# A fused two-block kernel: how the first four feed-forward units follow the second norm

## The reference, cut to what matters

```
x = x + gt_a * rmsnorm_2(mix @ w_out[l], g_post_attn[l])

h = rmsnorm_2(x, g_pre_ffn[l]) * (1.0 + sc_f) + sh_f
f = (jax.nn.silu(h @ w_gate[l]) * (h @ w_up[l])) @ w_down[l]
x = x + gt_f * rmsnorm_2(f, g_post_ffn[l])
```

## Time and the profile before

| | us |
|---|---|
| median of 3 runs (lowest, highest) | 3028.91 (3028.78, 3029.4) |
| profiled execution, own time | 3028.81 |
| its span | 3027.1 |
| TensorE busy in it | 3009.3 (99%) |
| VectorE busy | 2268.5 (75%) |
| ScalarE busy | 1244.6 (41%) |
| GpSimd busy | 361.5 (12%) |

### The profile page before, as it was taken

The page is one execution under the profiler, slowest core; times in us unless marked ns, Lnnn a source line. Parts: engine busy times, 40 slices in busy tenths (PEclk is TensorE's granted clock), DMA queues, the critical chain, the costliest instruction groups (busy, mean ns, idle before and its releaser), DMA issues.

```text
span 3027.1 us, 41400 instructions
## 1 busy us (share of the span) xinstructions
PE 3009.3 (99%) x15360; PEld 2532.1 (84%) x15360; DVE 2268.5 (75%) x2840; ACT 1244.6 (41%) x1596; POOL 361.5 (12%) x523
## 2 busy tenths in 40 slices
PE   9999999999999999999999999999999999999998
PEld 7888887888888888888888788888888888888887
DVE  7666656868887666788765798888888888888875
ACT  5332343213234333444442454444444444344433
POOL 0211100111110011010000200000000000011123
PEclk9999999999999999999999999999999999999999
DMA  5444453876764444444332366666666666578874
GB/s 193 151 127 133 136 196 135 322 261 232 263 250 169 162 166 167 146 154 154 138 140 97 119 180 171 179 178 176 180 173 170 173 168 179 186 228 229 229 228 158
DMA packets 121373, 544.43 MB, mean 180 GB/s; under 512 B 22496, under 2 KB 22768, under 8 KB 81584
## 3 DMA queue, kind: packets, MB, share of 16 engines
q1 hardware_dynamic: 64432, 321.15, 30.1%
q0 software_dynamic: 53088, 194.85, 23.3%
q10 hardware_dynamic: 3744, 26.98, 2.3%
HBM read 433.86 MB, written 37.49 MB: 156 GB/s over the span
## 4 chain that ended last, share of the span: by engine, by line
PE 98%; DVE 2%; DMA 0%; ACT 0%; issue 0%; DVEq 0%; SPq 0%; ACTq 0%
PE PS L2007 18%; PE PS L1553 15%; PE PS L1554 15%; PE PS L1555 15%; PE PS L2010 9%; PE PS L2077 3%; PE PS L2076 3%; PE PS L2074 3%; PE PS L2042 1%; PE PS L2044 1%; PE PS L2043 1%; PE PS L1876 1%; PE PS L1612 1%; PE PS L1614 1%; PE PS L1613 1%; PE PS L1864 1%
## 5 line engine op out<-in xcount | busy, mean ns | idle before, releaser
L1553 PE MATMUL PS<-XHL,WH 128*128 128x512 f32 x1952 | 765.0, 392 | 0.3 <-DVE BB L2581 0.3
L1555 PE MATMUL PS<-XHL,WL 128*128 128x512 f32 x1952 | 759.9, 389 | 0.0
L1554 PE MATMUL PS<-XHL,WH 128*128 128x512 f32 x1952 | 759.6, 389 | 0.0
L986 ACT ACTIVATE WH<-RAW 128x2048 fp32r<-128x2048 f32 x137 | 262.1, 1913 | 463.4 <-PE PS L1555 461.9
L1553 PEld LDWEIGHTS PS<-XHL,WH 128*128 128x128 f32 x1952 | 366.5, 188 | 80.7 <-issue 4.0
L1555 PEld LDWEIGHTS PS<-XHL,WL 128*128 128x128 f32 x1952 | 366.4, 188 | 76.5
L1554 PEld LDWEIGHTS PS<-XHL,WH 128*128 128x128 f32 x1952 | 366.6, 188 | 74.8 <-issue 0.2
L2093 DVE TENSOR_TENSOR WL<-RAW,WH 128x2048 fp32r<-128x2048 f32 x136 | 310.9, 2286 | 66.9 <-ACT WH L986 66.7
L1341 ACT ACTIVATE QH<-RAW 128x1024 fp32r<-128x1024 f32 x210 | 222.2, 1059 | 251.7 <-PE PS L2010 242.6
L2007 PE MATMUL PS<-XHL,QH 128*128 128x512 f32 x1008 | 316.6, 395 | 0.0
L2954 DVE TENSOR_TENSOR QL<-RAW,QH 128x1024 fp32r<-128x1024 f32 x210 | 256.6, 1222 | 58.6 <-ACT QH L1341 58.4
(11 more groups left out here) (446 smaller groups left out, 5277.2 us busy)
## 6 DMA issues: line engine op xcount, KB each, us to landing
RAW<-w_units_dram SPq DMA_DIRECT2D x228, 1024.0 KB, 4.9
ADA<-w_ada_dram POOLq DMA_DIRECT2D x112, 512.0 KB, 5.5
ADAQ<-w_ada_dram POOLq DMA_DIRECT2D x80, 512.0 KB, 5.6
A<-w_units_dram SPq DMA_DIRECT2D x32, 1024.0 KB, 7.8
SUM<-RAW POOLq DMA_DIRECT2D x42, 512.0 KB, 4.7
RAW<-SUM POOLq DMA_DIRECT2D x42, 512.0 KB, 4.5
FRAW<-f_dram SPq DMA_DIRECT2D x4, 2048.0 KB, 13.0
A<-A POOLq DMA_DIRECT2D x8, 1024.0 KB, 7.5
```

What stands on the lines that cost most here:

```text
L986: act.activation(WH[:, slot, :], RAW[:, slot, :], ACT.Copy).then_inc(hi_ready, 1)
L1553: pe.matmul(PS[:, bank, :], wh, rh[:, x, :], start=k == 0, stop=False)
L1554: pe.matmul(PS[:, bank, :], wh, rl[:, x, :], start=False, stop=False)
L1555: ins = pe.matmul(PS[:, bank, :], wl, rh[:, x, :], start=False, stop=k == n - 1)
```

## The change

Units 0, 1 and 2 run in step: tile k of unit 0, tile k - 1 of unit 1 and tile k - 1 of unit 2. Unit 2's weights move to slot 1 of `WH`/`WL` and are prepared during the norm; unit 3's move to `PAIRH`/`PAIRL` and are prepared in halves, and its output goes to bank 5. The tiles pass through three PSUM banks where there were four, so a norm step from tile 3 on also waits for ScalarE's copy of the tile three before it (`x_copied`). The `scaled_by_row` steps stand later: after the low step, and at other tiles (`SCALED_AT`). GpSimd makes the first combination of `RES`, in eight pieces of 128x256 behind its additions 8 to 15; VectorE makes the others in a new order. The saves of `BB` to DRAM go from ScalarE's queue to SP's, the table load for silu goes ahead of the tiles, one sum of the norm is folded on VectorE so that TensorE has four small matmuls fewer, and the second block of dummy matmuls has six instructions where it had four. SP loads the two weights of the second fast pair behind unit 3 instead of unit 1, the second of them behind GpSimd's first accumulating DMA.

```diff
@@ constants
+SCALED_AT = {1: (5, 7), 3: (7, 9), 6: (9, 11), 8: (11, 13), 10: (13, 16)}
-    XBANK = (2, 3, 4, 6)
+    XBANK = (3, 4, 6)
+    UPBANK = (1, 5)
@@ SP
+            x3_save(0, 4)
             for k in range(2):
+                if k == 1:
+                    for t0, t1 in ((4, 8), (8, 12), (12, 14), (14, 16)):
+                        x3_save(t0, t1)
                 sp.wait_ge(lo_ready, U_FFN + 3 + k)
                 sp.dma_start(RAWS[0][:, k, :], w_units[U_FFN + 2 * PLAIN + k]).then_inc(pair_loaded[0], 16)
-            sp.wait_ge(out_done, O_FFN + 2)
+            sp.wait_ge(out_done, O_FFN + 4)
             for k in (1, 0):
+                if k == 0:
+                    sp.wait_ge(later_sums, 16)
                 sp.dma_start(RAWS[1][:, k, :], w_units[U_FFN + 2 * PLAIN + 2 + k]).then_inc(pair_loaded[1], 16)
@@ GpSimd
                 gp.tensor_tensor(BB[:, t, :], BB[:, t, :], RES[:, t, :], ALU.add).then_inc(x3_ready, 1)
+                if t >= FULL_K:
+                    k = t - FULL_K
+                    gp.wait_ge(x_copied, k + 1)
+                    ins = gp.tensor_tensor(RES[:, k, LO], RES[:, k, LO], RES[:, k, HI], ALU.subtract)
+            ins.then_inc(t_sum, 1)
@@ ScalarE
+            act.activation(WH[:, 1, :], RAW[:, 0, :], ACT.Copy).then_inc(hi_ready, 1)
 ...
+            act.activation(SPARE, ONES[:, 0:1], ACT.Silu)
             for t in range(DT):
                 act.wait_ge(x_freed, DT + t + 1)
-                act.activation(XH[:, t, :], PS[:, XBANK[t % 4], :], ACT.Identity,
+                act.activation(XH[:, t, :], PS[:, XBANK[t % 3], :], ACT.Identity,
                                bias=MOD[:, 3 * DT + t:3 * DT + t + 1]).then_inc(xh_ready, 1)
                 if t >= 1:
-                    x_copied(t - 1)
-                if t % 4 == 3:
-                    act.wait_ge(x3_ready, t + 1)
-                    act.dma_start(x3_d[:, t - 3:t + 1, :], BB[:, t - 3:t + 1, :]).then_inc(saved, 16)
-            x_copied(DT - 1)
-            third_hi(act, U_FFN + 2, 2, 0)
-            act.activation(SPARE, ONES[:, 0:1], ACT.Silu)
+                    x_copy(t - 1)
+            fourth_hi(0)
+            x_copy(DT - 1)
@@ TensorE
-            token_sums(SIG[:, 1, :], 0, G2[:, DT - 1:DT], False, True, bank=4)
-            clocked(4, 0, O_OUT2 + DT - 1)
+            clocked(6, 0, O_OUT2 + DT - 1)
-            pair(U_FFN, O_FFN, X_FFN, True)
-            third(U_FFN + 2, O_FFN + 2, 3, 2, X_FFN)
-            unit(U_FFN + 3, 1, O_FFN + 3, [FULL], 3, 4, X_FFN)
+            for k in range(TILES + LAG):
+                if k < TILES:
+                    paired(0, k, U_FFN, X_FFN, own=True)
+                if k >= LAG:
+                    ins = paired(1, k - LAG, U_FFN, X_FFN, own=True)
+                    if k - LAG == TILES // 2 - 1:
+                        ins.then_inc(half_used, 1)
+                    if k == LAG:
+                        pe.wait_ge(half_lo, 7)
+                    if k - LAG == TILES // 2:
+                        pe.wait_ge(lo_ready, U_FFN + 3)
+                    ins = product(WH[:, 1, :], WL[:, 1, :], 2, k - LAG)
+            ins.then_inc(out_done, 1)
+            pe.wait_ge(half_lo, 8)
+            for k in range(TILES):
+                if k == TILES // 2:
+                    pe.wait_ge(lo_ready, U_FFN + 4)
+                ins = product(PAIRH, PAIRL, UPBANK[1], k)
+            ins.then_inc(out_done, 1)
@@ VectorE
-            scaled_by_row(5, 7)
+            home_lo(WH[:, 1, :], WL[:, 1, :], RAW[:, 0, :], 0, None)
             v.wait_ge(row_ready, 4)
             for t in range(DT + 1):
                 if t < DT:
                     v.wait_ge(x3_ready, t + 1)
+                    if t >= 3:
+                        v.wait_ge(x_copied, t - 2)
 ...
-                if t in (1, 3, 5):
-                    scaled_by_row(t + 6, t + 8)
-                if t == 7:
-                    scaled_by_row(13, 16)
                 if t >= 1:
 ...
+                if t in SCALED_AT:
+                    scaled_by_row(*SCALED_AT[t])
+                if t == 4:
+                    home_lo(WH[:, 1, :], WL[:, 1, :], RAW[:, 0, :], 1, U_FFN + 3)
+            home_lo(PAIRH, PAIRL, RAW[:, 1, :], 0, 6)
```

More of the change, by code:

```diff
@@ L411, in build @@
         saved, misc_loaded = sem("saved"), sem("misc_loaded")
+        x_copied, x3_saved = sem("x_copied"), sem("x3_saved")
         rope_ready, vt_ready, vtr_done, vs_ready, qk_done = (
@@ L421, in build @@
         x2_loaded = [sem(f"x2_loaded{c}") for c in range(4)]
[L422 to L425, removed]
+        last_square, prod_ready, u_ready = (sem(n) for n in ("last_square", "prod_ready", "u_ready"))
+        turn_ready, turn_saved, gate_moved, gained, root_ready, corner_scaled, corner_added = (
+            sem(n) for n in ("turn_ready", "turn_saved", "gate_moved", "gained",
                              "root_ready", "corner_scaled", "corner_added"))
@@ L1464, in _ @@
             ins.then_inc(t_hi, 1)
+            fourth_hi(1)
+            plain_silu(0)
             plain_silu(1)
@@ L1970, in _ @@
             token_sums(SIG[:, 1, :], 0, ONES[:, 0:1], False, True).then_inc(ms_ready, 1)
-            token_sums(ACCC, 0, ONES[:, 0:1], True, False, bank=4)
+            token_sums(ACCB, 4, ONES[:, 0:1], True, False, bank=4)
             token_rows(3, 0, 7)
-            token_sums(ACCB, 4, ONES[:, 0:1], False, False, bank=4)
-            token_sums(SIG[:, 1, :], 0, G2[:, DT - 1:DT], False, True, bank=4)
             pe.wait_ge(prod_ready, 1)
+            token_sums(ACCC, 0, ONES[:, 0:1], False, True, bank=4)
+            pe.wait_ge(prod_ready, 2)
             token_sums(PROD, 4, ONES[:, 0:1], False, True, bank=4).then_inc(ms_ready, 1)
@@ L2013, in fast_pair, with product @@
                     ins.then_inc(q_done, 1)
-            pair(U_FFN, O_FFN, X_FFN, True)
-            third(U_FFN + 2, O_FFN + 2, 3, 2, X_FFN)
-            unit(U_FFN + 3, 1, O_FFN + 3, [FULL], 3, 4, X_FFN)
+            def product(wh, wl, bank, x):
+                wh, wl = wh[:, x * P:(x + 1) * P], wl[:, x * P:(x + 1) * P]
+                pe.matmul(PS[:, bank, :], wh, XH[:, x, :], start=x == 0, stop=False, skip_group_check=True)
+                pe.matmul(PS[:, bank, :], wh, XL[:, x, :], start=False, stop=False, skip_group_check=True)
+                return pe.matmul(PS[:, bank, :], wl, XH[:, x, :], start=False, stop=x == TILES - 1,
+                                 skip_group_check=True)
+            for u in range(2):
+                pe.wait_ge(out_read, READ0 + O_FFN + u - 1)
+            for k in range(TILES + LAG):
[17 more added lines that the diff above has]
+            ins.then_inc(out_done, 1)
             with pe.Fori(0, LOOPED // 4) as i:
@@ L2890, in _ @@
                     modulation(V_GPF, 4 * DT)
+                    v.tensor_tensor(DS, MOD[:, 3 * DT:3 * DT + FULL_K], MOD[:, 3 * DT + FULL_K:4 * DT], ALU.subtract)
+            v.drain()
+            v.wait_ge(last_square, 1)
+            v.scalar_tensor_tensor(out=ACCC[:, :], in0=SIG[:, 1, :], scalar=G2[:, DT - 1:DT], in1=ACCC[:, :],
+                                   op0=ALU.mult, op1=ALU.add).then_inc(prod_ready, 1)
             v.wait_ge(out_read, READ0 + O_FFN)
@@ L2918, in _ @@
             tt(m, m, AE, ALU.add)
-            ts(e, m, EPS, None, ALU.max).then_inc(mean_ready, 1)
+            ts(e, m, EPS, None, ALU.max).then_inc(prod_ready, 1)
             scaled_by_row(4, 5)
@@ L2922, in _, with home_lo @@
             v.reciprocal(e, e).then_inc(scale_ready, 1)
-            scaled_by_row(5, 7)
+            def home_lo(hi, lo, raw, h, count):
+                part = slice(h * D // 2, (h + 1) * D // 2)
+                v.wait_ge(hi_ready if h or count is None else half_hi, U_FFN + 3 if count is None else count)
+                v.tensor_tensor(lo[:, part], raw[:, part], f32(hi[:, part]), ALU.subtract)\
+                 .then_inc(lo_ready if h else half_lo, 1)
+            home_lo(WH[:, 1, :], WL[:, 1, :], RAW[:, 0, :], 0, None)
             v.wait_ge(row_ready, 4)
@@ L3107, in _, with third_t @@
             ins.then_inc(t_lo, 1)
+            def third_t(tiles):
+                for t in tiles:
+                    m = 3 * DT + FULL_K + t
+                    ins = v.scalar_tensor_tensor(out=TC[:, t, hi], in0=RES[:, FULL_K + t, hi], scalar=MOD[:, m:m + 1],
+                                                 in1=f32(TC[:, t, lo]), op0=ALU.add, op1=ALU.subtract)
+                return ins
+            lo_part(0, 0, 0, 0)
             sum_3(0, 32)
-            lo_part(0, 0, 0, 0)
+            sum_1(0)
             lo_part(0, 0, 1, 1)
-            sum_1(0)
+            lo_part(0, 0, 2, 2)
+            plain_hidden(0)
             plain_hidden(1)
             v.drain().then_inc(copied, 1)
-            lo_part(0, 0, 2, 2)
             lo_part(0, 0, 3, 3)
             v.wait_ge(t_hi, 3)
-            for t in range(FULL_K):
-                m = 3 * DT + FULL_K + t
```

(4 more changed lines are left out.)

57 lines of the change are left out of this document (30 added, 27 removed).

## The result

| | before | after |
|---|---|---|
| median, us (lowest to highest, 20 runs each) | 3029.02 (3028.58 to 3029.63) | 3032.93 (3031.37 to 3034.82) |
| ratio after / before, 95% interval | | 1.0013 (1.0007 to 1.0019) |
| span of the profiled execution | 3027.1 | 3031.3 |

A forecast was written before the change was run, and what follows sets the result against it. The prediction took TensorE as the bound, busy 3009.3 of 3027.1 us. From the profiled 3028.81 it subtracted 3.6 for the earlier first fast pair and took all else at 0: 3025.2, range 3024.0 to 3028.0.

The forecast's parts named there:

- The first fast pair earlier by 3.6: With three units in step, the first fast pair starts at 1760.8 us instead of 1764.39.
- The wait between tile 0 and tile 1: TensorE's waits on the low step shrink from 4.7 to about 1.5 us, nearly all between these tiles.
- No wait for later tiles: VectorE just keeps up until tile 10, with margin nil at tile 4, so TensorE waits for no later tile.
- GpSimd's pieces: Each half-width subtraction behind additions 8 to 15 takes 0.65 us, between nothing and 1.24, and stays hidden.
- (a): Rival, tiles late: GpSimd's pieces cost as much as an addition, or weight halves wait for additions; 3026 to 3027.6, chance 0.16.
- (d): Rival, slower: GpSimd's last piece gates `TA` high, unit 3's weights and so product 0; 3029 to 3036, chance 0.08.
- The VectorE half against GpSimd: The first half of unit 2's low part, both inputs in SBUF, waits 0.2 us for a GpSimd addition; 0 on the path.
- The second pair's weights: Loads and accumulating DMAs for the second fast pair arrive in time: 0.2 us lost at most, taken as 0.
- rival (b): Second pair late: load and accumulating DMAs slow each other beyond 5.6 and 9.2 us; 3025.7 to 3028.2, chance 0.11.
- The DMA takes 4.5 to 5.6: The second accumulating DMA, sent together with a weight load, takes 4.5 to 5.6 us and lands at 1773.8.
- high and low part of product 6 to 1776.3: Product 6's operand in the first fast pair is ready at 1776.3 us, wanted at 1777.5, margin 1.2.
- Each microsecond more costs one: If the second pair's load and accumulating DMAs are late, each microsecond of delay lengthens the run by one.

The follow-up runs named there:

- e3: The changed kernel with the second pair's two loads cut in halves, first halves sent when unit 3 is half done, none behind an accumulating DMA: 3026.8 us, ratio 0.9993.
- e4: The changed kernel with the first pair's second sum made by VectorE instead of GpSimd's accumulating DMA, a tiny DMA carrying its count: 3027.35 us, ratio 0.9994.
- e7: The changed kernel with both weight loads of the second pair behind the first accumulating DMA: 3035.52 us, ratio 1.0021.
- e1: The changed kernel with the bank read ahead of product 6's low part and `sum_3` in every fast pair: 3031.21 us, ratio 1.0007.
- e8: The changed kernel with the 256 KB save ahead of the second pair's second load: 3032.39 us, ratio 1.0011.
- e5: The changed kernel with e3's half loads, e1's earlier bank read, and the save behind the second accumulating DMA: 3026.43 us, ratio 0.9991.
- e6: The kernel before with only its four `scaled_by_row` steps among the tiles moved behind the low step: 3029.11 us, ratio 1.0.
- e2: The changed kernel with both weight loads of the second pair sent when unit 3 ends: 3031.36 us, ratio 1.0008.

## Why the prediction was wrong

**Right.** The first fast pair earlier by 3.6: 4.24 in the trace, 3.9 of it from the change. The wait between tile 0 and tile 1: 1.42, forecast 1.5 for all tile waits. No wait for later tiles, though VectorE had no margin at tile 4: the last low step ended at 1741.3 (forecast 1742.3). GpSimd's pieces took 0.74 (forecast 0.65), the last began at 1738.99 (forecast to end by 1740), so rivals (a) and (d) did not come. The VectorE half against GpSimd, forecast to wait 0.2, took 1.51 for 1.22:

```profile
1710.89 1.51 DVE L2984 TENSOR_TENSOR WL<-RAW,WH 128x1024 fp32r<-128x1024 f32 x1
...
1757.82 1.23 DVE L3020 TENSOR_TENSOR QL<-RAW,QH 128x1024 fp32r<-128x1024 f32 x1 [1.15 <-ACT QH L1369]
```

The second of these rows is product 0's low part: done at 1759.05, forecast 1759.3, 1.1 before TensorE wants it.

**Wrong: the step "The second pair's weights", taken at 0.** Three terms of it failed, and the measured price was 6.66 up to product 6 and 1.75 for the clock; the mechanism is rival (b), to which I gave 0.11 and at most 3028.2. The bank read and the clock stand in none of the rivals.

- *"The DMA takes 4.5 to 5.6".* That range came from 42 `sum_4` with other neighbours. I let the load grow with company, up to 9.2, and not the accumulating DMA that goes out beside it. It took 9.5, and it is the one on the path. e3 and e4 take its delay away in two ways and give 6.1 and 5.5 us back. `sum_2` was forecast at 5.2 and took 6.4. The waits of 0.43 and 0.29 at products 4 and 5 hang on it, for which the prediction worked out no margin and foretold no wait on `QL`: in e7, with `sum_2` at 5.1, only 0.26 is left of them.
- *"high and low part of product 6 to 1776.3", wanted at 1777.5.* Product 6 also waits for the bank read, which stands on VectorE behind its low part and `sum_3`. That is 1.7 more: ready at 1776.3 + 1.7 = 1778.0 for 1777.5, a margin of -0.5 where I had 1.2, before any DMA was late. With the DMA on time its own price is 0.3 (e3).
- *"Each microsecond more costs one".* Behind the 5.26 wait the clock was at half for 3.9 us, and that cost 1.75 beyond the wait; behind e1's 3.30 and e8's 3.68 it cost 1.7 and 2.9. The waits of 1.42 at 1717.08 and 1.1 in e4 cost nothing of the kind.

The sum with these terms: 3028.81 - 4.24 + 6.66 + 1.75 = 3032.98, for 3033.02 in the profiled run. All three terms are read from that run, so this says that nothing else was lost, and does not test the causes; e1, e3 and e4 do.

**What stays of the gain.** e3 has the start of the fast pairs at 1760.5, 3.9 earlier, and ends 2.0 earlier. Between product 0 and 6 it loses 1.7: waits of 0.7 and 0.3, and some 0.7 for the three restarts. TensorE has caught up with the weight sums of the first pair, so the last microsecond of an earlier start is not to be had without moving these too; that is argued from the rows, and no run tried it.

**Open.** Which of the load, the save and the loop's next load costs `sum_4` how much is known only in steps of the table: no kernel had the second load alone beside it. The larger spread of the changed kernel (3.45 us for 1.05) goes with the long wait: 2.5 to 5.4 in all kernels that kept it, 1.3 to 2.2 in e3, e4 and e5. The clock, which took 1.7 to 2.9 behind waits of 3.3 to 5.9, may be part of it; no run tried that. Why the clock fell behind 1.43 in e6 and not behind 1.42 in the changed kernel is open too.

## What to carry to other kernels

When an edit makes the bound engine arrive earlier, list everything that it meets at the new time: each product's operands, the bank it writes, and what stands ahead of each of these in its engine's list. The margin of the last one in the chain counts, not of the first. If two transfers are set off by one event, price both with the other running, and take the row of the slow one for whichever is on the path; here splitting the loads and sending the first halves 5 us earlier was worth 6 us (e3 against the changed kernel). The stalls of 3.3 to 5.9 us in TensorE cost 1.7 to 2.9 more than their length, so a forecast of a late operand needs a second term.

## What the runs showed of the hardware

- A 512 KB accumulating DMA from SBUF to SBUF takes 4.5 to 5.6 us alone and up to 10.7 beside two 1 MB loads and a save: about twice.
- After idle times of 3.3 to 5.9 us in the middle of dense work the granted clock read about 0.5 for 3 to 6 us; in e1 only from about 1.3 us after the restart. The price beyond the wait, counted in groups of four matmuls from the restart on, did not grow with the wait: 1.7 behind 3.30 (e1), 2.9 behind 3.68 (e8), 1.7 behind 4.29 (e2), 1.75 behind 5.26 (the changed kernel), 2.1 behind 5.86 (e7).
- Shorter waits went both ways. Behind 1.65 in the kernel before and 1.42 in the changed one the clock read 1.00. In e6 it fell to 0.50 behind 1.43, which came three matmuls after a wait of 0.72.
- A wait of TensorE costs about 0.25 us more than the profile prints for it. The matmuls of 128x512 take 0.39 each but start 0.23 apart; at the 0.79 wait they started 1.18 apart, which is 0.39 + 0.79, and the overlap was missing.
